# A third place for split weights, and what moves with it, in a two-block transformer kernel on one core

## The chip, the cores and the metric

The kernel runs on one core of one Trainium2 chip. The metric is the device time of one execution in microseconds (us). One execution takes about 2.1 ms. TensorE (PE) multiplies, VectorE (DVE) and ScalarE (ACT) work elementwise, GpSimd (POOL) does little here, SyncE (SP) does nothing but wait and issue transfers. The five run from their own instruction lists, in order, and meet at semaphores.

## The reference, cut to what matters

Float32 in and out, 256 tokens of 2048 channels. The first block is a mixer, a cross attention and a mixture of 16 experts. The second block has two layers, and most of the change lies in them:

```python
for l in range(2):
    mod = silu(c) @ w_ada[l] + b_ada[l]            # 2048 x 6144: a product with one row
    shift, scale, gate = split(mod, 3)
    h = rmsnorm(x, norm_g[l]) * (1 + scale) + shift
    z = h @ w_in[l]                                # 2048 x 6656: 13 pieces of 512
    o_fft  = fourier_mix(f_x, w_fft[l]) * silu(f_g)
    o_na   = neighbourhood_attention(na_q, na_k, na_v, bias[l]) * silu(na_g)
    o_ret  = retention(rotary(r_q), rotary(r_k), r_v) * silu(r_g)
    o_cv   = conv31_layernorm_silu(cv_a, cv_b) @ w_pw[l] * silu(cv_g)
    x = x + gate * (concat(o_fft, o_na, o_ret, o_cv) @ w_out[l])

def rotary(t):                                     # t1, t2: the halves of a head of 64
    return concat(t1 * cos - t2 * sin, t1 * sin + t2 * cos)
```

## The kernel before, in words

**Blocks of weights.** Every large product runs over blocks of 128 x 2048 float32 (1 MB). SP loads a block into one of four raw places (`raw`, rooms 0 to 3, line 471). ACT writes its high half as float16 (line 644), DVE the low half (line 1292, which also gives the raw place back, `raw_taken`), and PE multiplies x-high by w-high, x-low by w-high and x-high by w-low: 48 matmuls for a block (line 2241). The halves have two places (`SPL = 2`, `w_hi`, `w_lo`), so ACT may start on block m only when PE is done with block m - 2 (`block_done`).

**The order of the stream.** `STREAM` lists the phases: `w_in` (40 blocks), `w_out`, `wk`, `wq`, `wv`, `wo` (16 each), `moe` (192 blocks, in rings of their own and up to eight raw places), then for each of the two layers `z` (52 blocks, 4 for each of the 13 pieces in `Z_ORDER`) and `mix` (16). `raw_rooms` (line 125) gives each block the raw place that was used longest ago. Two small weight matrices of a layer sit in the same stream and hold a raw place unsplit until PE has used them: `w_fft` after block 43 of `z`, used at block 45 (`fft_map`, lines 2805 to 2818), and `conv_w_pw` after block 48 (`small`, line 2839).

**The modulation units.** The product with `w_ada` is done on DVE: 12 units of 16 steps, each step 128 x 1024 float32 (0.5 MB), loaded by SP into one of two staging buffers (line 476, `load_ada`, which waits until the step two before is used) and added with one instruction of DVE (line 1263). `ada_plan` (line 144) says after which block a step comes. In `z` the steps of the first unit come after blocks 2 to 13 and those of the second unit after the blocks up to 29. DVE does a step right behind its split of that block, inside `split` (line 1285). SP's list is fixed too: load of block m, then the steps that belong to block m - 2 (`load_due(2)`, line 482), then, after block 43, `w_fft`.

**What else DVE and PE do within `z`.** DVE applies 120 taps of the convolution (`TAPS_AT`, line 2008), the attention's maxima, the rotary of q and k (`rotary`, line 2038, blocks 28, 30, 32, 34), weights of the retention, `conv_centre` at 41, `conv_squares` at 42, `na_gate` and `fft_weights` (lines 2076, 2101, 2102) at 43, `conv_norm` and `mixed_lo` (lines 2068 to 2071 and 2124) at 44. PE does `rotate(j)` (line 2740: a float32 product with a 128 x 128 permutation, into bank 2 of `GB`), scores, transposes and small products between the blocks; at 45, ahead of the block, it does `ret_square_sum` (line 2773) and `fft_map`.

**Start of the experts.** PE gathers the sorted rows in 16 products, DVE copies the low part of each (line 1867), ACT the high part (line 976), and the first expert's product takes them one by one.

Of the kernel before, what the change touches and what calls it, by code (L numbers as in the profile page):

```python
# [14 lines left out]
P = 128  # L15
T = 256
# [8 lines left out]
SPL = 2  # L25
# [24 lines left out]
Z_UNITS = (7, 8, 10, 11)  # L50
# [4 lines left out]
TAPS_AT = {**{m: 4 for m in range(11, 20)}, 20: 6, 21: 3, 22: 5, 23: 6, 24: 3, 25: 5, 26: 6, 27: 3, 28: 3, 29: 6, 30: 2,  # L55
           31: 6, 32: 2, 33: 6, 34: 3, 35: 4, 36: 4, 37: 4, 38: 7}
# [5 lines left out]
def constants():  # L62
# [13 lines left out]
    out["rope_cos"], out["rope_sin"] = np.cos(rope), np.sin(rope)  # L76
    rot = np.zeros((P, P))
    for m in range(P):
        if m % DH < half:
            rot[m + half, m] = -1.0  # L80
        else:
            rot[m - half, m] = 1.0
    out["rot"] = rot
# [41 lines left out]
def raw_rooms():  # L125

    (first, _, n), total = places()["moe"], sum(n for _, n, _ in STREAM)
    rooms, uses, last = [], [0] * ROOMS, [-1] * ROOMS
    for b in range(total):
        j = b - first  # L130
        open_ = list(range(RAW))
        if 0 <= j < n:
            open_ += [4] * (j >= 6) + [5] * (7 <= j < 126) + [6] * (j >= 7) + [7] * (13 <= j < 150)
        r = min(open_, key=lambda r: last[r])
        uses[r], last[r] = uses[r] + 1, b
        rooms.append((r, uses[r]))
    return rooms
# [6 lines left out]
def ada_plan():  # L144
# [21 lines left out]
    fast("z0")  # L166
    for m in [2, 2, 3, 4, 4, 5, 6, 6, 7, 8, 8, 9, 9, 10, 10, 11]:
        put("mix0", m)
    fast("z1")
# [27 lines left out]
def build(nc, A, table, const_at, columns, router, out):  # L197
    ctx = ExitStack()
    with ctx:
# [21 lines left out]
        w_hi = sb("w_hi", [P, SPL, BLK], F16)  # L221
        w_lo = sb("w_lo", [P, SPL, BLK], F16)
# [30 lines left out]
        hid_at = [H[:, k * 1024:(k + 1) * 1024] for k in range(4)] + [Zf[:, c * T:c * T + 1024] for c in (28, 48)] + [Yf[:, k * 1024:(k + 1) * 1024] for k in range(2)]  # L253
        raw_at = [raw[:, r, :] for r in range(RAW)] + [w3, Yf[:, 0:BLK], Yf[:, BLK:2 * BLK], Zf[:, 40 * T:48 * T]]
# [32 lines left out]
        RO = Y[:, 5:7, :]  # L287
        f_parts = w2[:, 0:1024].rearrange("p (a k g n) -> p a k g n", a=TT, k=2, g=4)
        f_last = w2[:, 1024:1032].rearrange("p (a g) -> p a g", a=TT)
# [8 lines left out]
        LO_AT = {"ga": 0, "weight": KC, "t": KC + 1, "y": KC + 1 + 4 * TILES}  # L298
# [61 lines left out]
        def ada_sums(u):  # L360
            if u in Z_UNITS:
                return Zf[:, (4 * (u in (8, 11))) * T:(4 * (u in (8, 11)) + 4) * T]
# [13 lines left out]
        def ada_bank(u):  # L376
            return MB[:, 0, 0:8] if u in (8, 11) else GB[:, 2, 0:8]
# [42 lines left out]
        def done(eng, ph, j, i=0):  # L420

            s = where(ph, j)[1]
            eng.wait_ge(block_done[s % SPL], s // SPL + 1 + 2 * i)
# [31 lines left out]
        def _(sp):  # L455
# [5 lines left out]
            def load(ph, j, src):  # L461
                r, n = rooms[where(ph, j)[0]]
                if n > 1:
                    sp.wait_ge(raw_taken[r], n - 1)
                elif r == 4:
# [12 lines left out]
            ADA_ROOM = {"w_out": ("hgrn_y", 2), "z0": ("norm_ms", 4), "mix0": ("small_mm", 2), "z1": ("norm_ms", 5)}  # L478

            due = []  # L480

            def load_due(depth):

                while len(due) > depth:
# [3 lines left out]
                    for step in steps:  # L488
                        load_ada(step)
# [66 lines left out]
        def _(gp):  # L556
# [64 lines left out]
        def _(act):  # L621
            def split_half(ph, j, half):
# [7 lines left out]
                act.activation(w_hi[:, s % SPL, cut], raw_at[r][:, cut], ACT.Copy, scale=W_SCALE).then_inc(hi_done, 1)  # L630

            def split(ph, j, i=0):
# [3 lines left out]
                if ph == "moe":  # L636
                    act.wait_ge(block_done[s % SPL], s // SPL - 1)
# [3 lines left out]
                else:  # L641
                    act.wait_ge(block_done[s % SPL], s // SPL + 2 * i)
                    w = w_hi[:, s % SPL, :]
# [369 lines left out]
            for n in range(MOE_STEPS):  # L1013
                f, last = n // 8, n % 8 == 7
                for part in range(2):
# [19 lines left out]
                    if n == 2 and part == 1:  # L1035
# [205 lines left out]
        def _(dve):  # L1241
# [23 lines left out]
            def ada_add(u):  # L1265
                dve.wait_ge(ada_mm, u + 1)
                mod = MOD[:, u // 6, u % 6 * 8:u % 6 * 8 + 8]
                if u % 6 < 4:
# [5 lines left out]
                    ("z0", 20): 7, ("z0", 33): 8, ("mix0", 14): 9, ("z1", 20): 10, ("z1", 33): 11}  # L1274

            def split_half(ph, j, half):
# [4 lines left out]
                ins = dve.scalar_tensor_tensor(w_lo[:, s % SPL, cut], raw_at[rooms[b][0]][:, cut], W_SCALE, w_hi[:, s % SPL, cut], ALU.mult, ALU.subtract)  # L1281
# [3 lines left out]
            def split(ph, j, i=0):  # L1285
                b, s = where(ph, j)
                dve.wait_ge(hi_done, s + 1 + 4 * i + (s > at["z1"][1]))
                hi, lo = w_hi[:, s % SPL, :], w_lo[:, s % SPL, :]
# [576 lines left out]
            def gather_lo(c):  # L1865
                dve.wait_ge(S("moe_mm"), MM_AT["ga"] + c + 1)
                dve.tensor_copy(xs_lo[:, c, :], gather_bank(c, 1)).then_inc(S("moe_lo"), 1)  # L1867
# [32 lines left out]
            for n in range(MOE_STEPS):  # L1900
                f, last = n // 8, n % 8 == 7
                for part in range(2):
# [23 lines left out]
                    if part == 1:  # L1926
                        if n == 0:
                            groups_left()
                        if n == 2:
# [3 lines left out]
                        if n in (3, 4):  # L1933
                            place_rows(n - 3)
# [41 lines left out]
            for l in range(LAYERS):  # L1976
# [244 lines left out]
        def _(pe):  # L2221
            def product(ph, j, b, k0, start, stop, groups=None, x=(xh, xl), rows=False, between=None):

                s = at[ph][1] + j
                hi = w_hi[:, s % SPL, :].rearrange("p (c n) -> p c n", c=8)
                lo = w_lo[:, s % SPL, :].rearrange("p (c n) -> p c n", c=8)
# [767 lines left out]
```

## Time and profile before

| what | us |
|---|---|
| median of 3 runs | 2095.44 |
| lowest and highest run | 2094.69, 2101.43 |
| the profiled execution: its own time | 2093.71 |
| its span, first to last instruction | 2091.7 |
| PE busy | 2041.4 |
| DVE busy | 1752.3 |
| ACT busy | 1194.1 |

The span is 2.0 us shorter than the profiled execution's own time, and that is 1.7 us under the median. The stages in the trace: `w_in` 17 to 266 us, `w_out` to `wo` until 725, experts 725 to 1233, `z` of the first layer 1247 to 1573, its `mix` to 1660, `z` of the second layer 1667 to 1994, its `mix` to 2078. Busy times are unions; the idle time of an engine stands with what ended it, as the trace infers it from the semaphores.

### The profile page before, as it was taken

The numbers are of one execution on the slowest core, as the hardware profiler recorded it, in microseconds if no ns is written. First come the engines' busy times: TensorE is split into PE (matmuls) and PEld (weight loads), VectorE is DVE, ScalarE is ACT, GpSimd is POOL, SyncE is SP. The second block draws the span as 40 slices with busy tenths as digits, with TensorE's granted clock in tenths as the row PEclk, the third lists the DMA queues.
The fourth block names the chain that finished last, engine by engine and source line by source line (L and its number), as shares of the span: only waits on it lengthen the run. The fifth ranks groups of instructions, "written<-read, shape, count | busy, mean of one in ns | idle before, by whom it ended". The sixth has DMA issues, their size and how long they took to land.

```text
span 2091.7 us, 42599 instructions
## 1 busy us (share of the span) xinstructions
PE 2041.4 (98%) x18993; PEld 1641.1 (78%) x18993; DVE 1752.3 (84%) x1670; ACT 1194.1 (57%) x1071; POOL 41.3 (2%) x40
## 2 busy tenths in 40 slices
PE   8999999999999989999999999999999899999998
PEld 7889888888889946555556568888888788888887
DVE  7875787988888799999999999999668779996555
ACT  5554644444445478877877864456554444565543
POOL 0002300000000000000000000000000000000000
PEclk9999999999999999999999999999999999999999
DMA  8854487789888878999999987874458778744452
GB/s 303 317 202 162 163 314 271 280 307 326 319 326 298 309 280 355 420 420 420 420 420 416 408 318 293 294 256 164 143 184 310 281 286 304 250 162 159 181 202 101
DMA packets 95717, 593.23 MB, mean 284 GB/s; under 512 B 10664, under 2 KB 10824, under 8 KB 36784
## 3 DMA queue, kind: packets, MB, share of 16 engines
q1 hardware_dynamic: 94912, 583.73, 74.4%
q0 software_dynamic: 624, 6.80, 0.8%
q8 instruction: 149, 2.44, 0.5%
q14 instruction: 32, 0.26, 0.0%
HBM read 588.39 MB, written 2.10 MB: 282 GB/s over the span
## 4 chain that ended last, share of the span: by engine, by line
PE 68%; DVE 16%; DMA 10%; ACT 3%; issue 3%; DVEq 0%; SPq 0%; POOL 0%; ACTq 0%; POOLq 0%
PE GB L2241 52%; DVE w_lo L1292 6%; PE GB L2670 4%; DVE W L1292 3%; PE MB L2670 3%; DMA raw<-w_up 3%; DMA W<-w_ada 2%; ACT w_hi L644 2%; DMA Z<-w_ada 2%; DMA raw<-w_down 2%; DVE W L1263 1%; DVE Z L1263 1%; DMA raw<-w_gate 1%; PE MB L2839 1%; PE MB L2441 1%
## 5 line engine op out<-in xcount | busy, mean ns | idle before, releaser
L644 ACT ACTIVATE w_hi<-raw 128x2048 f16<-128x2048 f32 x308 | 588.1, 1910 | 705.5 <-PE GB L2241 680.9
L1292 DVE SCALAR_TENSOR_TENSOR w_lo<-raw,w_hi 128x2048 f16<-128x2048 f32 x308 | 706.0, 2294 | 244.9 <-ACT w_hi L644 244.2
L2241 PE MATMUL GB<-H,w_hi 128*128 128x256 f16 x4352 | 718.9, 273 | 18.3 <-DVE w_lo L1292 11.6
L2241 PE MATMUL GB<-H,w_lo 128*128 128x256 f16 x2176 | 593.8, 273 | 0.0
L2241 PEld LDWEIGHTS GB<-H,w_hi 128*128 128x128 f16 x4352 | 421.6, 98 | 85.0 <-DVE w_lo L1292 16.6
L2241 PEld LDWEIGHTS GB<-H,w_lo 128*128 128x128 f16 x2176 | 213.2, 98 | 24.9
L2241 PE MATMUL GB<-w_hi,H 128*128 128x256 f16 x1280 | 210.7, 273 | 0.0
L1263 DVE SCALAR_TENSOR_TENSOR W<-W,SM 128x1024 f32<-128x1024 f32 x120 | 153.8, 1282 | 31.8 <-DMA W<-w_ada 28.5
L2241 PE MATMUL GB<-w_lo,H 128*128 128x256 f16 x640 | 174.4, 273 | 0.0
L2241 PE MATMUL GB<-Z,w_hi 128*128 128x256 f16 x1024 | 170.0, 274 | 2.9 <-DVE w_lo L1292 2.9
L2241 PE MATMUL GB<-W,w_hi 128*128 128x256 f16 x1024 | 168.0, 273 | 2.7 <-DVE w_lo L1292 2.7
L2241 PE MATMUL GB<-Z,w_lo 128*128 128x256 f16 x512 | 140.4, 274 | 0.0
L2241 PE MATMUL GB<-W,w_lo 128*128 128x256 f16 x512 | 139.6, 273 | 0.0
L2241 PEld LDWEIGHTS GB<-w_hi,H 128*128 128x128 f16 x1280 | 124.7, 98 | 16.1 <-issue 1.3
L1292 DVE SCALAR_TENSOR_TENSOR W<-raw,W 128x2048 f16<-128x2048 f32 x54 | 123.2, 2286 | 2.3 <-ACT W L644 2.2
L644 ACT ACTIVATE W<-raw 128x2048 f16<-128x2048 f32 x54 | 103.0, 1911 | 20.9 <-DMA raw<-w_down 6.1
L2241 PEld LDWEIGHTS GB<-Z,w_hi 128*128 128x128 f16 x1024 | 100.4, 98 | 16.0 <-DVE w_lo L1292 3.8
L2241 PEld LDWEIGHTS GB<-W,w_hi 128*128 128x128 f16 x1024 | 99.9, 98 | 14.9 <-DVE w_lo L1292 3.3
L2008 DVE SCALAR_TENSOR_TENSOR Y<-Y,PC 128x256 f32<-128x256 f32 x240 | 99.6, 479 | 0.0
L2670 PE MATMUL GB<-W,Z 128*64 (+1 forms) x864 | 86.7, 353 | 4.4 <-DVE Z L1867 4.3
L2670 PE MATMUL MB<-W,Z 128*64 (+1 forms) x864 | 86.0, 353 | 1.3 <-DVE W L1292 1.2
L1263 DVE SCALAR_TENSOR_TENSOR Z<-Z,SM 128x1024 f32<-128x1024 f32 x60 | 76.8, 1281 | 10.7 <-DMA Z<-w_ada 9.9
(489 smaller groups left out, 2789.9 us busy)
## 6 DMA issues: line engine op xcount, KB each, us to landing
raw<-w_in SPq DMA_DIRECT2D x144, 1024.0 KB, 5.2
W<-w_ada SPq DMA_DIRECT2D x128, 512.0 KB, 5.6
raw<-w_out SPq DMA_DIRECT2D x48, 1024.0 KB, 5.1
raw<-w_down SPq DMA_DIRECT2D x41, 1024.0 KB, 10.6
raw<-w_gate SPq DMA_DIRECT2D x34, 1024.0 KB, 11.0
raw<-w_up SPq DMA_DIRECT2D x32, 1024.0 KB, 12.8
Z<-w_ada SPq DMA_DIRECT2D x64, 512.0 KB, 5.9
raw<-xattn_wk SPq DMA_DIRECT2D x16, 1024.0 KB, 5.1
```

The costliest lines, as they stand in the source:

```text
L644: act.activation(w, raw_at[r], ACT.Copy, scale=W_SCALE).then_inc(hi_done, 1)
L1263: dve.scalar_tensor_tensor(sums, w, SM[:, 24 + k:25 + k], sums, ALU.mult, ALU.add).then_inc(ada_used[n % 2], 1)
L1292: dve.scalar_tensor_tensor(lo, raw_at[r], W_SCALE, hi, ALU.mult, ALU.subtract).then_inc(raw_taken[r], 1)
L2008: dve.scalar_tensor_tensor(ca[:, c, :], CU[:, c, k // 4:k // 4 + T], col("conv_w_2", l * TAPS * 4 + k), ca[:, c, :], ALU.mult, ALU.add).th ...
L2241: last = pe.matmul(o, a, m, start=first, stop=end and w_part is lo, skip_group_check=True)
L2441: ins = pe.matmul(MB[:, h % 2, a * T:a * T + T], x_q[q][:, 4 * h + c, a * P:a * P + P], x_k[k][:, 4 * h + c, :], start=a == 0 and c == 0 a ...
L2670: ins = pe.matmul(o_bank(j, k)[r:r + SLOT], x[:, c0 + c, at_:at_ + SLOT], v, start=kh == 0 and c == 0 and part == 0, stop=kh == 7 and c == ...
L2839: ins = pe.matmul(banks[:, n // 2, n % 2 * T:n % 2 * T + T], w[:, k, n * P:n * P + P], x[:, k, :], start=n % 2 == 0 and k == 0, stop=k == ...
```

## The change

1. `SPL = 3`: the halves get a third place. It is cut out of raw place 3, so outside the experts the blocks of the stream use raw places 0 to 2 only; within the experts place 3 opens at the fifth block. ACT may now start on block m when PE is done with block m - 3.
2. The steps of each `z`'s second modulation unit move from blocks 14 to 29 to blocks 35 to 46; those of the first unit are spread up to block 16. The products that finish the units move to blocks 19 and 50. Staging and sums of the second unit get other buffers (`w2`, `w3`), and the spectrum's parts move from `w2` to `w1`.
3. The taps are dealt out again over blocks 11 to 37 (120 as before).
4. The rotary partner is moved by POOL: four transfers of 32 partitions x 512 float32 for each of the four pairs of pieces, in place of `rotate`. The sign goes into the table of sines. DVE's three instructions stay, the first reads SBUF in place of PSUM.
5. At the start of the experts ACT copies the low part of the odd gathers, DVE only of the even ones; `groups_left`, `best_two` and `place_rows` come a step or two later.

```diff
-SPL = 2
+SPL = 3
-Z_UNITS = (7, 8, 10, 11)
+Z_UNITS = (7, 10)
-TAPS_AT = {**{m: 4 for m in range(11, 20)}, 20: 6, 21: 3, 22: 5, 23: 6, 24: 3, 25: 5, 26: 6, 27: 3, 28: 3, 29: 6, 30: 2,
-           31: 6, 32: 2, 33: 6, 34: 3, 35: 4, 36: 4, 37: 4, 38: 7}
+TAPS_AT = {11: 5, 12: 4, 13: 6, 14: 4, 15: 6, 16: 4, 17: 6, 18: 6, 19: 6, 20: 6, 21: 6, 22: 2, 23: 6, 24: 6, 25: 2, 26: 6, 27: 6, 28: 2, 29: 4, 30: 6, 32: 6, 33: 2, 34: 6, 35: 2, 36: 3, 37: 2}
...
-        open_ = list(range(RAW))
+        open_ = list(range(RAW - 1))
         if 0 <= j < n:
-            open_ += [4] * (j >= 6) + [5] * (7 <= j < 126) + [6] * (j >= 7) + [7] * (13 <= j < 150)
+            open_ += [3] * (j >= 4) + [4] * (j >= 6) + [5] * (7 <= j < 126) + [6] * (j >= 7) + [7] * (13 <= j < 150)
...
-    def fast(ph):
-        for m in [2 + 2 * k // 3 for k in range(13)] + list(range(11, 30)):
+    def halves(ph):
+        for m in [2, 2, 3, 4, 4, 5, 6, 6, 7, 8, 8, 9, 10, 12, 14, 16]:
+            put(ph, m)
+        for m in [35, 36, 37, 37, 38, 39, 39, 40, 41, 41, 42, 42, 43, 44, 45, 46]:
             put(ph, m)
...
+        third = raw[:, RAW - 1, :].bitcast(F16)
+        hi_of = [w_hi[:, 0, :], w_hi[:, 1, :], third[:, 0:BLK]]
+        lo_of = [w_lo[:, 0, :], w_lo[:, 1, :], third[:, BLK:2 * BLK]]
...
+                for j in range(4):
+                    for u in range(j % 2 + 1):
+                        gp.wait_ge(bank_free[u], uses[f"z{l}"][u] + 6 + j // 2)
+                    if j == 0:
+                        gp.wait_ge(S("tap"), 4 * TAPS * l + 4)
+                    if j == 3:
+                        gp.wait_ge(S("rotated"), 4 * l + 1)
+                    if l or j:
+                        gp.wait_ge(S("rot"), 64 * (4 * l + j))
+                    for d in range(0, P, DH // 2):
+                        s = d ^ DH // 2
+                        gp.dma_start(RO[j % 3][d:d + DH // 2], Z[s:s + DH // 2, 24 + 2 * j:26 + 2 * j, :]).then_inc(S("rot"), 16)
...
             def gather_hi(c):
                 act.wait_ge(S("moe_mm"), MM_AT["ga"] + c + 1)
+                if c % 2:
+                    act.activation(xs_lo[:, c, :], gather_bank(c, 1), ACT.Copy)
                 act.activation(xs_hi[:, c, :], gather_bank(c, 0), ACT.Copy).then_inc(S("moe_hi"), 1)
...
                 def rotary(j):
                     x = Z[:, 24 + 2 * j:26 + 2 * j, :]
-                    dve.wait_ge(S("rot"), 4 * l + j + 1)
-                    link(dve.tensor_tensor(RO, GB[:, 2, :].rearrange("p (c t) -> p c t", t=T), sin, ALU.mult))
+                    dve.wait_ge(S("rot"), 64 * (4 * l + j + 1))
+                    ro = RO[j % 3]
+                    link(dve.tensor_tensor(ro, ro, sin, ALU.mult))
                     link(dve.tensor_tensor(x, x, cos, ALU.mult))
-                    dve.tensor_tensor(x, x, RO, ALU.add).then_inc(S("rotated"), 1)
+                    dve.tensor_tensor(x, x, ro, ALU.add).then_inc(S("rotated"), 1)
...
-                def rotate(j):
-                    evicted(pe, l, 5 + j // 2)
-                    if j == 0:
-                        pe.wait_ge(ada_mod, 8 + 3 * l)
-                    else:
-                        pe.wait_ge(S("rotated"), 4 * l + j)
-                    pe.matmul(GB[:, 2, :], const("rot"), Z[:, 24 + 2 * j:26 + 2 * j, :].rearrange("p c t -> p (c t)"), start=True, stop=True).then_inc(S("rot"), 1)
-
...
-                    if m == 17:
+                    if m == 19:
                         ada_columns(7 + 3 * l)
-                    if m == 32:
-                        pe.wait_ge(S("na_max"), 8 * l + 8)
+                    if m == 50:
+                        pe.wait_ge(S("fft_act"), 7 * l + 7)
                         ada_columns(8 + 3 * l)
-                    for j in nth(m, 27, 2):
-                        rotate(j)
```

## Rows read from the trace of the kernel before

**Rows 1.** The page: busy time of each engine, share of the span, instructions.

```profile
PE 2041.4 (98%) x18993; PEld 1641.1 (78%) x18993; DVE 1752.3 (84%) x1670; ACT 1194.1 (57%) x1071; POOL 41.3 (2%) x40
```

**Rows 2.** Waits of PE, whole span: who waited for whom, total, times, longest.

```profile
PE GB L2241 <- DVE w_lo L1292: 17.3, 20, 2.1
PE GB L2670 <- DVE Z L1867: 5.2, 5, 1.6
```

**Rows 3.** The same view, 0 to 50 us.

```profile
PE GB L2241 <- DVE w_lo L1292: 2.8, 3, 1.9
```

**Rows 4.** The same view, 265 to 280 us.

```profile
PE GB L2241 <- DVE w_lo L1292: 2.1, 1, 2.1
```

**Rows 5.** Chain that ended last, around blocks 43 to 46: start, us, what.

```profile
1510.17 0.43 PE GB L2829 x2
1510.60 10.48 PE GB L2241 x96
1521.08 1.72 PE MB L2773 x4
...
1528.17 0.66 PE GB L2818 x4
1528.83 0.14 issue
1528.96 10.64 PE GB L2241 x96
```

**Rows 6.** SP's list in order of time, at the end of `fft_map`.

```profile
1528.84 0.80 SPq L471 DMA_DIRECT2D raw<-w_in  x2
```

**Rows 7.** ACT in order of time, within block 41.

```profile
1491.74 0.43 ACT L1140 ACTIVATE NS<-GB 128x256 f32<-128x256 f32 x1
1496.14 1.91 ACT L644 ACTIVATE w_hi<-raw 128x2048 f16<-128x2048 f32 x1 [3.97 <-PE GB L2241]
```

**Rows 8.** DVE in order of time, blocks 42 to 45.

```profile
1500.30 0.68 DVE L1995 TENSOR_TENSOR Z<-Y 128x512 f32<-128x512 f32 x1
1501.02 0.42 DVE L1996 TENSOR_TENSOR Z<-Z 128x256 f32<-128x256 f32 x1
1503.33 2.29 DVE L1292 SCALAR_TENSOR_TENSOR w_lo<-raw,w_hi 128x2048 f16<-128x2048 f32 x1 [1.89 <-ACT w_hi L644]
1505.54 0.42 DVE L2059 COPY Z<-GB 128x256 f32<-128x256 f32 x1
...
1508.26 1.23 DVE L2102 TENSOR_TENSOR raw<-raw 128x1024 f32<-128x1024 f32 x1
...
1514.42 1.75 DVE L2068 RECIPROCAL NS<-NS 128x256 f32<-128x256 f32 x1
...
1519.89 2.28 DVE L1292 SCALAR_TENSOR_TENSOR w_lo<-raw,w_hi 128x2048 f16<-128x2048 f32 x1
```

**Rows 9.** Line 476, 352 to 381 us, `w_ada` loads close behind a block's.

```profile
DMA to landing us min/median/max: 3.5/5.7/6.5
```

**Rows 10.** Line 476 again, 1262 to 1325 us.

```profile
DMA to landing us min/median/max: 3.5/5.2/7.8
```

**Rows 11.** Line 1263: engine, count, duration min/median/max in ns.

```profile
L1263 DVE SCALAR_TENSOR_TENSOR Z<-Z,SM x60: 1275/1280/1286, 1263.9 to 1835.7; 128x1024 f32<-128x1024 f32 x60
```

**Rows 12.** Stretches: length, busy of PE, PEld, DVE, ACT, POOL, clock, DMA.

```profile
36.24:38.18 1.94, 0.01 (x1) 0.01 (x1) 1.94 (x2) 1.93 (x3) 0.00 (x0) 1.00 1.01 416
38.62:42.03 3.41, 3.41 (x18) 2.35 (x16) 3.29 (x3) 0.82 (x3) 0.00 (x0) 0.50 0.99 393
270.91:272.96 2.05, 0.00 (x1) 0.00 (x0) 2.05 (x2) 2.02 (x3) 0.00 (x0) 1.00 0.00 0
274.14:277.54 3.40, 3.40 (x18) 2.44 (x17) 3.40 (x3) 0.92 (x1) 0.61 (x1) 0.50 0.84 341
```

**Rows 13.** Chain that ended last, 1402 to 1412 us: one rotation.

```profile
1402.54 0.86 PE GB L2740 x2
```

**Rows 14.** Line 1867: the copies of the gathered low parts.

```profile
L1867 DVE CAST Z<-MB x16: 616/618/625, 735.8 to 789.9; 128x448 f16<-128x448 f32 x16
```

**Rows 15.** Stretches: blocks 22 to 34, 35 to 45 of `z`, and two in the experts.

```profile
1368.00:1456.00 88.00, 87.43 (x770) 72.47 (x767) 86.93 (x127) 53.36 (x87) 0.00 (x0) 1.00 0.58 200
1456.00:1529.00 73.00, 72.85 (x620) 61.04 (x618) 52.22 (x55) 44.69 (x46) 0.00 (x0) 1.00 0.37 127
...
930.00:1230.00 300.00, 291.71 (x2960) 166.59 (x2958) 285.64 (x155) 241.06 (x159) 0.00 (x0) 1.00 1.01 414
```

**Rows 16.** POOL's small transfers (line 564): issue in ns, then landing.

```profile
L564 POOL DMA_DIRECT2D LG<-ret_logit_fwd x1: 555/555/555, 10.6 to 10.6; - x1
...
DMA to landing us min/median/max: 7.0/7.2/7.4
```

**Rows 17.** DVE in order of time: the last rotation's first instruction.

```profile
1446.79 0.68 DVE L2041 TENSOR_TENSOR Y<-GB,CT 128x512 f32<-128x512 f32 x1
```

More of the change, by code:

```diff
@@ L75, in constants @@
     rope = (t.astype(np.float32)[None, :] * inv[p % half][:, None]).astype(np.float32)
[L76 to L80, printed above, removed]
-        else:
-            rot[m - half, m] = 1.0
-    out["rot"] = rot
+    out["rope_cos"], out["rope_sin"] = np.cos(rope), np.sin(rope) * np.where(p % DH < half, -1.0, 1.0)[:, None]
     d = t[None, :] - t[:, None]
@@ L165, in ada_plan @@
         put("wo", m)
-    fast("z0")
+    halves("z0")
     for m in [2, 2, 3, 4, 4, 5, 6, 6, 7, 8, 8, 9, 9, 10, 10, 11]:
         put("mix0", m)
-    fast("z1")
+    halves("z1")
     assert count[0] == 12 * ADA_STEPS
@@ L220, in build @@
         raw = sb("raw", [P, RAW, BLK])
-        w_hi = sb("w_hi", [P, SPL, BLK], F16)
-        w_lo = sb("w_lo", [P, SPL, BLK], F16)
+        w_hi = sb("w_hi", [P, 2, BLK], F16)
+        w_lo = sb("w_lo", [P, 2, BLK], F16)
         XT = sb("XT", [P, KC, T])
@@ L286, in build @@
         ca, csq, cs = Y[:, 12:16, :], Y[:, 8:12, :], Z[:, 12:14, :]
-        RO = Y[:, 5:7, :]
-        f_parts = w2[:, 0:1024].rearrange("p (a k g n) -> p a k g n", a=TT, k=2, g=4)
-        f_last = w2[:, 1024:1032].rearrange("p (a g) -> p a g", a=TT)
+        RO = [Y[:, 5 + 2 * k:7 + 2 * k, :] for k in range(3)]
+        f_parts = w1[:, 0:1024].rearrange("p (a k g n) -> p a k g n", a=TT, k=2, g=4)
+        f_last = w1[:, 1024:1032].rearrange("p (a g) -> p a g", a=TT)
         f_cos, f_nyq, f_sin = Zf[:, 0:2 * MIRROR], Zf[0:4, 2 * MIRROR:3 * MIRROR], Zf[:, 2 * T:2 * T + 2 * MIRROR]
@@ L376, in ada_bank @@
         def ada_bank(u):
-            return MB[:, 0, 0:8] if u in (8, 11) else GB[:, 2, 0:8]
+            return MB[:, 0, 0:8] if u in Z_UNITS else GB[:, 2, 0:8]
         def na_p(h):
@@ L464, in load @@
                     sp.wait_ge(raw_taken[r], n - 1)
+                elif r == RAW - 1:
+                    done(sp, "wo", 13)
                 elif r == 4:
@@ L488, in load_due @@
                     for step in steps:
+                        if step in LATE_ROOM:
+                            sp.wait_ge(S("na_o"), LATE_ROOM[step])
                         load_ada(step)
@@ L629, in split_half @@
                 cut = slice(half * BLK // 2, half * BLK // 2 + BLK // 2)
-                act.activation(w_hi[:, s % SPL, cut], raw_at[r][:, cut], ACT.Copy, scale=W_SCALE).then_inc(hi_done, 1)
+                act.activation(hi_of[slot(s)][:, cut], raw_at[r][:, cut], ACT.Copy, scale=W_SCALE).then_inc(hi_done, 1)
             def split(ph, j, i=0):
@@ L636, in split @@
                 if ph == "moe":
-                    act.wait_ge(block_done[s % SPL], s // SPL - 1)
+                    act.wait_ge(block_done[(s - 4) % SPL], (s - 4) // SPL + 1)
                     if j < 2:
@@ L641, in split @@
                 else:
-                    act.wait_ge(block_done[s % SPL], s // SPL + 2 * i)
-                    w = w_hi[:, s % SPL, :]
+                    act.wait_ge(block_done[s % SPL], s // SPL)
+                    if (ph, j) == ("z0", 0):
+                        given_up(act, RAW - 1)
+                    w = hi_of[slot(s)]
                 act.activation(w, raw_at[r], ACT.Copy, scale=W_SCALE).then_inc(hi_done, 1)
@@ L1034, in _ @@
                             turned_hi(n // 16 - 1, k)
-                    if n == 2 and part == 1:
+                    if n == 3 and part == 1:
                         act.wait_ge(S("r_exp_in"), 1)
@@ L1926, in _ @@
                     if part == 1:
-                        if n == 0:
+                        if n == 2:
                             groups_left()
-                        if n == 2:
+                        if n == 3:
                             best_two()
@@ L1932, in _ @@
                             combine()
[L1933 to L1934 removed]
+                        if n in (4, 6):
+                            place_rows(n // 2 - 2)
                     if n == 6 and part == 1:
```

35 lines of the change are left out of this document (19 added, 16 removed).

## The prediction, made before the changed kernel ran

> **What bounds the kernel now.** I read the engines' shares first: PE is busy for 98% of the span, and its clock is at full speed in all but a few stretches [rows 1]. So a microsecond taken off PE's own list is a microsecond of the time, and a microsecond by which something keeps PE waiting is one too. Next the waits of PE: the largest entry is its wait for the low halves that DVE makes, 17.3 us in 20 waits, and after it 5.2 us for DVE's copies of gathered rows [rows 2]. Then the chain that ended last, in `z`: PE runs blocks of 48 matmuls in 5.24 us with small products between them, and nothing else is on it [rows 5]. DVE has 98% of blocks 22 to 34 filled, but only 72% of blocks 35 to 45 [rows 15]. Last I followed SP's list against the raw places, for the change takes one of four away.
>
> **Part 1, the rotations leave PE.** Each takes 0.86 us of PE's chain [rows 13], eight of them: 6.9 us off. DVE keeps its three instructions. The partner now comes by POOL's queue: four issues of 0.56 us and a landing of at most 7.4 us, so some 9.6 us a round by the nearest rows [rows 16]. Four rounds are 38 us. ACT gives the first piece away at about 1386 and the fourth at about 1418; the last round lands about 1428 and DVE wants it at 1446.8 [rows 17], or a block (5 us) earlier if it runs ahead. Cover: 13 us. Price taken: nothing.
>
> **Part 2, the third place of halves.** With two places a split may be late by 0.9 us at most: block 5.24, less 1.91 for the high half, 2.29 for the low half and the hand-overs [rows 5, 7, 8]. With three it may be late by 6.2 us. The 17.3 us of waits hold two that have other causes: 2.8 us at the start, where the norm feeds the blocks [rows 3], and 2.1 us at 271, where ACT stands behind a gate's result [rows 4]. That leaves 12.4 us. After each of the 16 waits PE takes a little to refill, so I take 14 us off. The bounds: 6, if DVE's lateness behind `w_ada` data comes back in part, and 17.
>
> **Part 3, the experts' start.** DVE loses eight copies of 0.62 us [rows 14] and PE its 5.2 us of waits for them at most [rows 2]. Most of the experts' stage runs at 414 GB/s with the transfers at their limit [rows 15], so an early start only counts as far as the transfers start early too. I take 3 us off, between 0 and 5.2.
>
> **Part 4, the moved unit.** Sixteen steps of 1.28 us [rows 11] leave the stretch in which DVE is 98% full for one with 21 us free in 73 [rows 15]; 20.5 us more there is less what the taps took with them (12 taps fewer). As work it fits. As an order of waits it does not, and this is where I put the time. Follow the raw places. With three, each block's load waits for the split of the block three ahead of it in the stream, and `w_fft` counts as a block that is given back only when `fft_map` ends. So block 46 follows `w_fft`. SP's list has the steps of block 44 behind the load of block 46, those of 43 behind 45, those of 42 behind 44. And since `w_fft` lies between, loads 44 and 45 wait for the splits of blocks 42 and 43, the very ones behind which DVE waits for the steps' data. Before, no step came after block 29, so nothing hung on this; in before's trace it is the load of block 47 that goes out as `fft_map` ends, at 1528.84 [rows 5, 6].
>
> *Block 44.* In before's times: ACT is free at 1492.2 [rows 7]; 1.9 for the high half, 2.3 for the low, so block 42 is split at 1496.4. Load 44 goes, the two steps' loads follow 0.4 us behind, and land 5.7 us later [rows 9]: 1502.5. Two steps: 1505.1. The squares' sums, 1.1: 1506.2. Split 43: 1508.5. Again 6.1 us and one step: 1515.9. Then the copy, gate and `w_fft` sums, in before 1505.5 to 1509.5, 4.0 us: 1519.9. Split 44: 1522.2 [rows 8, 11]. PE wants block 44 at 1515.9 [rows 5]. PE waits 6.3 us. Bounds 1.9 (landings of 3.5 us [rows 9]) and 8.
>
> *Block 45.* `fft_map` ends, load 46 goes out, and 0.4 us behind it the step of block 44. It lands at 6.1 us, the step ends at 7.4; only then may DVE do the norm of the convolution and the low part behind it, in before 1514.4 to 1519.9, 5.5 us, and then split 45, 2.3 [rows 8, 9, 11]. PE, which in before goes straight on at 1528.96 [rows 5], waits 15.0 us. Queued behind that step on DVE are all these; on SP, behind the blocked load 46, are loads 47, 48 and `conv_w_pw`; by my walk they come in time. Bounds 12.8 and 17.1, by landings of 3.5 and 7.8 us [rows 10]. Both waits come in both layers: 2 x 21.3 = 42.6 us on.
>
> *The clock.* After PE had stood still for 1.94 and for 2.05 us its granted clock fell from 1.00 to 0.50 (2.4 to 1.2 GHz) for 3.41 and 3.40 us [rows 12], which costs half of that, 1.7 us. Four long waits: 6.8 us on; bounds 3.4 and 13.6.
>
> **The sum** against the profiled execution: 2093.7 - 6.9 - 14 - 3 + 42.6 + 6.8 = 2119.2, rounded to 2119 (the median of the runs shown is 1.7 above that execution, which is within the rounding of the terms). The low ends together: 2093.7 - 6.9 - 17 - 5.2 + 29.4 + 3.4 = 2097. The high ends: 2093.7 - 6.9 - 6 + 0 + 50.2 + 13.6 = 2145.
>
> **Rivals.** *A, the room does not bind.* The loads of blocks 44 to 46 and the steps behind them come in time, because the given-back places run ahead of what I walk through. For it: PE in before had no wait at all in blocks 35 to 46 [rows 15], and the third place lets splits run a block early. Against it: no early split helps a load that waits for `fft_map`. Then only the gains stand: 2093.7 - 23.9 = 2070. It decides where the two waits of a layer fall below 12 us together: from there the gains win. *B, POOL's transfers are late.* DVE is busy for 86.9 of 88 us there [rows 15], and if that holds up POOL's transfers, a round takes longer than by the rows of the kernel's start. It binds from about 15 us a round; at 19 us the last lands 16 us too late, in both layers: 2119 + 32 = 2151. The Trainium skill has the mechanism (SBUF — State Buffer, section "SBUF: two separate sides"): it says that GpSimd cannot write the descriptors of its own transfers while certain VectorE instructions hold the port pair that they share. No run here shows it for the rotary. *C, the third place gives nothing*, because DVE's lateness comes from the `w_ada` data itself, two staging buffers deep, and three raw places let SP issue those a block later: 2119 + 14 = 2133. *D, the change doesn't act as described*, for instance the halves' third place is never free in time, with nothing lost: 2095.
>
> **Chances.** Forecast (both waits in both layers, gains as taken) 0.66; A 0.12; B 0.05; C 0.13; D 0.04. C lies within the forecast's bounds, so does most of what could shift a term. I leave A and B out: the range is 2097 to 2141. A measurement of this kernel can tell about 0.3%, 6 us, from no change. Faster by more than that: A, 0.12. Within it: D and the low corner of the forecast, 0.07. Slower: 0.81.
>
> **What would show it.** In the changed profile: no line 2740, and 0.86 us less at four places of each `z`; PE's waits for the low halves in `w_in` to `wo` and in `mix` near nothing; in each `z` a wait of PE of some 6 us ahead of block 44 and some 15 us ahead of block 45, ended by DVE's split, with DVE waiting ahead of line 1263's instruction for a `w_ada` transfer issued just after `fft_map`; the granted clock at 0.50 behind each. If PE is without a wait there, the walk along the raw places is wrong and the time is near 2070. If DVE waits ahead of the rotation's first instruction, it is B.

## The result, and the profile after

The changed kernel took 2198.0 us (median of four runs, 2196.0 to 2203.8) against 2095.1 us: a ratio of 1.049, 95% interval 1.046 to 1.052. The direction and the place of the long waits were as forecast; the size was four times as large, +103 us where +24 had been forecast, and far outside the range of 2097 to 2141 us.

The profiled execution took 2203.8 us, 110 more than the one of before. The page, part 1 (busy time of each engine, its share of the span, instructions), beside [rows 1]:

```profile
PE 2061.3 (94%) x18977; PEld 1645.2 (75%) x18977; DVE 1751.7 (80%) x1662; ACT 1196.0 (54%) x1079; POOL 58.1 (3%) x72
```

PE lost its share of the span, DVE did the same work as before (1752 us). PE was busy 20 us longer with 16 instructions fewer, at a mean granted clock of 0.976 where it had been 0.994. The other 90 of the 110 us are idle time of PE: it waited. Whom PE waited for (total, times, longest), beside [rows 2]:

```profile
PE GB L2266 <- DVE w_lo L1315: 72.5, 41, 15.0
PE GB L2266 <- DVE raw L1315: 31.7, 16, 15.1
```

Both lines are the same split on DVE; the third place of halves lies in `raw`, hence the second name. Together 104 us, where 17.3 had been. What did the splits wait for? The same view of DVE, first for after, then for before:

```profile
DVE W L1286 <- DMA W<-w_ada: 198.9, 82, 21.6
DVE Z L1286 <- DMA Z<-w_ada: 33.2, 20, 3.7
```

```profile
DVE W L1263 <- DMA W<-w_ada: 28.5, 33, 1.8
DVE Z L1263 <- DMA Z<-w_ada: 9.9, 9, 2.7
```

In these lines DVE stood still for `w_ada` data for 232 us where it had been 38. The question is where this reached PE. The table takes the stretches between the ends of blocks' last matmuls in the two profiled executions, in us (the first column up to block 39 of `w_in`, the experts up to their last block):

```
                   w_in  w_out..wo  experts  z:0-20   21-35   36-42   43-45   46-51   mix
before  layer 0   265.7      459.3    508.3   131.8    96.0    49.1    24.2    38.7   87.4
after   layer 0   272.4      479.7    510.6   141.3    91.4    49.1    56.1    39.1   94.5
before  layer 1                               125.0    96.2    49.1    24.2    39.2   83.8
after   layer 1                               133.3    91.4    49.1    57.1    39.1   83.8
```

Blocks 43 to 45 lost 31.9 and 32.9 us: that is the place of the forecast. But `w_in` to `wo` lost 27 us (1.2 of them before the first block's end, with no step near), blocks 0 to 20 of `z` lost 9.5 and 8.3, and `mix` of layer 0 lost 7.1: 52 us in stages from which the forecast took its gain. The last `mix` has no step of `w_ada`, and it is the same to 0.1 us. Only blocks 21 to 35 gained, 4.6 and 4.8 us. Blocks 36 to 42 have eleven steps since the change and lost nothing: with the small products between them PE takes 7.0 us for a block there (49.1 for seven), not 5.24.

**Blocks 43 to 45** look as the walk along the raw places said. DVE in order of time (start, us, line, operation; in brackets the idle time before it and who ended it):

```profile
1541.04 2.69 DVE L1286 SCALAR_TENSOR_TENSOR W<-W,SM 128x1024 f32<-128x1024 f32 x2 [6.30 <-DMA W<-w_ada]
...
1544.71 2.28 DVE L1315 SCALAR_TENSOR_TENSOR w_lo<-raw,w_hi 128x2048 f16<-128x2048 f32 x1
1554.73 1.28 DVE L1286 SCALAR_TENSOR_TENSOR W<-W,SM 128x1024 f32<-128x1024 f32 x1 [7.74 <-DMA W<-w_ada]
...
1559.80 2.28 DVE L1315 SCALAR_TENSOR_TENSOR w_lo<-raw,w_hi 128x2048 f16<-128x2048 f32 x1
1583.67 1.28 DVE L1286 SCALAR_TENSOR_TENSOR W<-W,SM 128x1024 f32<-128x1024 f32 x1 [21.59 <-DMA W<-w_ada]
1584.88 1.74 DVE L2093 RECIPROCAL NS<-NS 128x256 f32<-128x256 f32 x1
...
1590.35 2.28 DVE L1315 SCALAR_TENSOR_TENSOR raw<-raw 128x2048 f16<-128x2048 f32 x1
```

These are the splits of blocks 43, 44 and 45, each with a late step ahead of it. The third step's data were sent for just after `fft_map` had ended. SP's list in order of time:

```profile
1547.02 0.33 SPq L475 DMA_DIRECT2D raw<-w_in  x1
1547.39 0.43 SPq L480 DMA_DIRECT2D W<-w_ada  x1
1577.60 0.33 SPq L475 DMA_DIRECT2D raw<-w_in  x1
1577.98 0.43 SPq L480 DMA_DIRECT2D W<-w_ada  x1
```

PE's longest waits in these stretches (layer 0, then layer 1):

```profile
PE GB L2266 <- DVE raw L1315: 15.1, 1, 15.1
PE GB L2266 <- DVE w_lo L1315: 11.2, 2, 9.7
```

```profile
PE GB L2266 <- DVE w_lo L1315: 21.4, 2, 15.0
PE GB L2846 <- DVE Z L2020: 3.6, 1, 3.6
```

**Everywhere else** the same thing happens in small. `w_out`, DVE:

```profile
296.03 2.28 DVE L1315 SCALAR_TENSOR_TENSOR w_lo<-raw,w_hi 128x2048 f16<-128x2048 f32 x1
298.51 2.69 DVE L1286 SCALAR_TENSOR_TENSOR W<-W,SM 128x1024 f32<-128x1024 f32 x2 [0.20 <-DMA W<-w_ada]
301.11 2.28 DVE L1315 SCALAR_TENSOR_TENSOR raw<-raw 128x2048 f16<-128x2048 f32 x1
306.38 1.28 DVE L1286 SCALAR_TENSOR_TENSOR W<-W,SM 128x1024 f32<-128x1024 f32 x1 [2.98 <-DMA W<-w_ada]
...
308.18 2.28 DVE L1315 SCALAR_TENSOR_TENSOR w_lo<-raw,w_hi 128x2048 f16<-128x2048 f32 x1
```

and SP:

```profile
298.34 0.33 SPq L475 DMA_DIRECT2D raw<-w_out  x1
299.82 0.33 SPq L480 DMA_DIRECT2D W<-w_ada  x1
303.42 0.33 SPq L475 DMA_DIRECT2D raw<-w_out  x1
```

Read it as a ring. The split of block 4 ends at 298.31 and gives its raw place back. At 298.34 the load of block 7, three ahead, goes out. Behind it stands the step of block 5; its transfer is issued at 299.82, when a staging buffer comes free too, and DVE starts on the data at 306.38. The step is done at 307.7, and the split of block 6 ends at 310.46. That is two blocks in 12.15 us, where PE needs 10.48 for two. The stretch (length, busy of PE, PEld, DVE, ACT, POOL, clock, DMA share, GB/s):

```profile
298.31:310.46 12.15, 10.65 (x96) 9.31 (x96) 8.86 (x7) 3.42 (x3) 0.00 (x0) 1.00 0.78 278
```

PE stood still for 1.5 of the 12.15 us and DVE for 3.3, so no engine was the bound: the ring itself was. In before, with four places, the same ring goes from a split to the third one after it and has three blocks' time, 15.7 us.

### The profile page after: what moved, and what is told of

It reads as the page before. It is cut to its first block, busy times and chain, and to the rows that moved or that the text cites. A ratio compares the mean times of both kernels' runs of the same rounds, so it can differ in the third digit from the quotient of the medians.

```text
span 2202.0 us, 42604 instructions
## 1 busy us (share of the span) xinstructions
PE 2061.3 (94%) x18977; PEld 1645.2 (75%) x18977; DVE 1751.7 (80%) x1662; ACT 1196.0 (54%) x1079; POOL 58.1 (3%) x72
## 4 chain that ended last, share of the span: by engine, by line
PE 27%; DVE 27%; DMA 26%; issue 16%; ACT 4%; SPq 1%; POOLq 0%; POOL 0%; DVEq 0%; ACTq 0%
PE GB L2266 16%; DMA W<-w_ada 14%; DVE w_lo L1315 8%; DVE W L1286 4%; DMA Z<-w_ada 4%; PE GB L2695 3%; PE MB L2695 3%; DVE W L1315 3%; DMA raw<-w_up 3%; DVE raw L1315 3%; DMA raw<-w_down 2%; ACT w_hi L665 2%; DMA raw<-w_gate 1%; DVE Z L1286 1%; DVE Y L2032 1%
## 5 line engine op out<-in xcount | busy, mean ns | idle before, releaser
L1315 DVE SCALAR_TENSOR_TENSOR w_lo<-raw,w_hi 128x2048 f16<-128x2048 f32 x223 | 511.1, 2295 | 80.8 <-ACT w_hi L665 79.9
L665 ACT ACTIVATE w_hi<-raw 128x2048 f16<-128x2048 f32 x223 | 425.0, 1906 | 209.9 <-PE GB L2266 97.6
L2266 PE MATMUL GB<-H,w_hi 128*128 128x256 f16 x2880 | 482.5, 275 | 51.0 <-DVE w_lo L1315 48.9
L2266 PE MATMUL GB<-H,w_lo 128*128 128x256 f16 x1440 | 395.4, 275 | 0.0
L2266 PEld LDWEIGHTS GB<-H,w_hi 128*128 128x128 f16 x2880 | 280.1, 99 | 98.5 <-DVE w_lo L1315 55.8
L2266 PE MATMUL GB<-H,raw 128*128 128x256 f16 x2208 | 257.1, 277 | 30.2 <-DVE raw L1315 26.8
L2266 PEld LDWEIGHTS GB<-H,raw 128*128 128x128 f16 x2208 | 217.3, 100 | 67.6 <-DVE raw L1315 31.0
L1315 DVE SCALAR_TENSOR_TENSOR raw<-raw 128x2048 f16<-128x2048 f32 x85 | 195.3, 2298 | 22.9 <-ACT raw L665 22.6
L665 ACT ACTIVATE raw<-raw 128x2048 f16<-128x2048 f32 x85 | 161.9, 1905 | 94.0 <-PE GB L2266 46.5
L2266 PEld LDWEIGHTS GB<-H,w_lo 128*128 128x128 f16 x1440 | 142.0, 99 | 17.4
```

The costliest lines, as they stand in the source:

```text
L665: act.activation(w, raw_at[r], ACT.Copy, scale=W_SCALE).then_inc(hi_done, 1)
L1315: dve.scalar_tensor_tensor(lo, raw_at[r], W_SCALE, hi, ALU.mult, ALU.subtract).then_inc(raw_taken[r], 1)
L2266: last = pe.matmul(o, a, m, start=first, stop=end and w_part is lo, skip_group_check=True)
```

## The experiments

Theory L ("the list"), formed after the result: what costs is how many blocks lie between the split that lets a load go and the split that waits for the `w_ada` data behind that load in SP's list. The change made them two instead of three. Ratios below are against the kernel before on the same chip, with their 95% interval.

**Three raw places alone.** `open_ = list(range(RAW - 1))` and `[3] * (j >= 4)` for the experts, the rest as before.

> The kernel before with three raw places outside the experts in place of four, and nothing else: two places of halves, its own plan of w_ada steps, its product for the rotary. Theory L (the list): a load waits for the low half of the block three back instead of four back, and the w_ada loads of the block two back stand behind it in SP's list, so they go out a block later; DVE, which wants them in order, waits for data, and its next low half is late. L expects DVE's waits for w_ada to grow from 41 us to over 150 us, PE's waits for low halves to grow from 17 us to some 60 us, and a time of 2140 to 2160 us. Rival H (the third place of halves or DVE's own work is what costs, not the raw place): the time stays within 6 us of the kernel before, 2095.

Measured: 2174.6 us, ratio 1.036 (1.033 to 1.040). A raw place alone costs more than L had said: PE's waits for low halves grew to 75 us, where L had said some 60. DVE's waits for `w_ada` data grew to 149 us, just under L's number. Rival H falls.

**Three raw places and three places of halves.** As above, with the changed kernel's `third`, `hi_of`, `lo_of` and `slot`.

> The kernel before with three raw places and three places of halves, nothing else of the change. L expects the third place of halves to give back some of what the raw place costs, since a late low half is covered by one block more of made halves: 2125 to 2145 us, clearly below the kernel with three raw places and two of halves, yet above the kernel before. The forecast's term (third place of halves gives 14 us off and the raw place costs nothing outside blocks 44 and 45) expects 2081 us. Rival H expects it no faster than the one with two places of halves.

Measured: 2167.6 us, ratio 1.034 (1.032 to 1.037), some 23 us above L's range. By the medians the third place of halves gave back 7 us, but the two intervals overlap, so a gain is not shown. The forecast's term (2081 us) is out. DVE waits for the steps' data no less than with two places of halves (149 us in these two lines, 144 there):

```profile
DVE W L1275 <- DMA W<-w_ada: 111.0, 68, 4.4
DVE Z L1275 <- DMA Z<-w_ada: 38.1, 31, 2.8
```

A likely reason, which no run tests by itself: a store of made halves covers a single late split, but where every pair of blocks takes longer than PE the store is soon empty.

**The order of SP's list, in the changed kernel.**

```diff
-                        load(ph, m, ...)
                         due.append((ph, plan.get(ph, {}).get(m, [])))
                         load_due(2)
+                        load(ph, m, ...)
```

> The changed kernel with one thing moved: SP issues the w_ada loads of the block two back ahead of a block's load instead of behind it, in every linear stage. L expects nearly all of the loss to go: the 27 us by the end of wo, the 65 us at blocks 44 and 45 of both layers and most of the 18 us in the first twenty blocks of z and in mix; 2080 to 2095 us, DVE's waits for w_ada under 60 us. A rival W (DVE's own work, or the two staging buffers of w_ada, hold the splits up) expects the waits to stay: 2170 us or more. A third, S (the loads of w_ada now hold up the loads of the blocks, since they wait for their staging buffers): 2110 to 2140 us.

Measured: 2095.3 us, ratio 1.000 (0.998 to 1.001). One line takes all of the 103 us away. The time lies 0.3 us above the range that L had named. PE's waits:

```profile
PE GB L2266 <- DVE w_lo L1315: 10.5, 7, 5.5
PE GB L2266 <- DVE raw L1315: 8.8, 4, 4.1
```

W falls (DVE's work and the two staging buffers are the same here), S too. L had DVE's waits for `w_ada` data wrong: it said under 60 us, and they are 93 us (81 in `W`, 11 in `Z`). PE's waits above show that most of them no longer reach it.

**The same only from block 42 of `z` on** (`late = ph in ("z0", "z1") and m >= 42`).

> The changed kernel with the same order of SP's list only from block 42 of each z on. L expects only the long waits ahead of blocks 44 and 45 to go, with the slow clock behind them: these two stretches were 64.8 us longer than in the kernel before, so 2133 us, and the rest of the loss, some 40 us, stays. If w_fft's place itself is what holds the stretch up (the load of block 46 after fft_map), the waits move to blocks 46 and 47 and the time is 2150 to 2175 us.

Measured: 2146.2 us, ratio 1.025 (1.021 to 1.028): 52 us off instead of 65. Blocks 43 to 45 are at 24.2 us again in both layers, as in before, so the waits there did hang on the list. The time lies between L's 2133 us and the 2150 of the other expectation, for both were at work. But blocks 46 to 51 took 47.2 and 45.0 us, against 38.7 and 39.2. That is the remark on `w_fft`'s place: PE now waited 5.6 and 4.1 us for block 46, whose load still goes out when `fft_map` ends. The kernel with three raw places alone, which has no step near, shows it too (44.9 and 45.0).

**The list changed by one number, with all four raw places.** The kernel before with `load_due(3)` for `load_due(2)`.

> The kernel before, all four raw places and two places of halves, with one number changed: SP issues the w_ada loads of a block behind the load of the block three further on, not two. Nothing is taken away, no work is added. L says that the raw place as such is not what matters, only how many blocks lie between the split that lets a load go and the split that waits for the w_ada data behind it: with four places and a distance of three these are two blocks, as with three places and a distance of two. L expects nearly the loss that the kernel with three places showed outside fft_map, some 65 us: 2150 to 2170 us. If a raw place less costs by the weights' own lateness (loads of blocks landing late), this kernel stays within 10 us of 2095.

Measured: 2164.8 us, ratio 1.031 (1.028 to 1.034), within what L said. Nothing was taken away and no work added; two blocks of distance do it. `w_out` to `wo` took 488.1 us (489.8 with three raw places alone, 459.3 before), blocks 46 to 51 of the first `z` 38.7 (44.9): the loss along the list is there, that at `w_fft`'s place is not. PE's and DVE's waits:

```profile
PE GB L2241 <- DVE w_lo L1292: 69.1, 62, 3.0
```

```profile
DVE W L1263 <- DMA W<-w_ada: 107.8, 69, 3.1
DVE Z L1263 <- DMA Z<-w_ada: 41.5, 31, 3.2
```

**Control: the new order in the kernel before.**

> The kernel before with only the order of SP's list changed, as a control: four raw places, two of halves. With four raw places each w_ada load already has three blocks of time; L expects 2090 to 2096 us, less only where DVE waited for w_ada data (41 us in all, most of them not on the path). If the new order is a gain by itself, whatever the places, it should show here as 2085 us or less, and then it is no proof for L.

Measured: 2096.0 us, ratio 1.000 (0.998 to 1.002), as L said. With four places the order is worth nothing that shows.

**Three raw places, three places of halves and the new order**, no other part.

> The kernel before with three raw places, three places of halves, and the w_ada loads ahead of the block's load in SP's list; no other part of the change. L expects the loss of the kernel with halves alone (72 us over the kernel before) to go in the stages with w_ada steps and the third place's gain to show there, some 12 us of PE's waits; what stays is the stretch after fft_map, which in the kernels with three raw places took about 6 us more per layer in blocks 46 to 51 with no w_ada step near, since the load of block 46 waits for w_fft's place. Together 2095 - 12 + 12 = 2095 us, 2088 to 2100. If the order were not the cause of the loss, 2150 us or more.

Measured: 2099.2 us, ratio 1.001 (1.000 to 1.002), within L's range and 68 us less than without the order. Against the control, `w_out` to `wo` are 2.5 us shorter and the first `mix` 3.2, while blocks 46 to 51 are 6.3 and 4.4 longer.

**The rotary by DMA alone**, on the kernel before.

> The kernel before with the rotary's partner moved by POOL's DMA in place of the product, and nothing else. The forecast's term: eight times 0.86 us, 6.9 us off, 2088 to 2089 us, if the transfers are hidden. The rival with POOL held up by DVE's instructions expects DVE to wait ahead of the rotation's first instruction and 2095 us or more.

Measured: 2096.6 us, ratio 1.001 (1.000 to 1.002): nothing, and neither expectation. The rival is out: DVE never sat idle ahead of the rotation's first instruction, in none of the eight rotations here and in none of the changed kernel's eight, and in the changed kernel the 32 transfers were issued in 0.50 us each and landed in 2.5 to 6.2 us. The products did leave PE. But blocks 21 to 35 took 95.3 and 95.5 us instead of 96.0 and 96.2, where four times 0.86 are 3.4. The stretch (length, busy of PE, PEld, DVE, ACT, POOL, clock, DMA share, GB/s):

```profile
1367.50:1462.70 95.20, 92.17 (x834) 78.15 (x831) 93.28 (x135) 58.24 (x88) 7.88 (x16) 1.00 0.62 215
```

DVE is busy for 93.3 of 95.2 us, PE for 92.2, and PE waited 2.1 us for a split at 1430. That DVE became the bound as soon as PE's list got shorter is argued from this row; the product put back, below, tests it.

**The gathers alone**, on the kernel before.

> The kernel before with every second low copy of the gathered rows on ACT and the router's work two steps later, and nothing else. The forecast's term was 3 us off, between 0 and 5.2: 2092 us. In the kernels run so far that had this part, the stretch from the end of wo to the last block of the experts was never shorter than before (508.2 to 510.6 us against 508.3). If what bounds that stretch is the transfers, an early start of PE gives nothing: 2095 us, within 0.2%.

Measured: 2092.7 us, ratio 0.998 (0.997 to 0.999), 3.8 us less by the medians and barely clear of nothing. The profiled execution does not say where: wo's end to the last experts' block is 508.6 us (508.3 before), and PE's waits for the low copies went from 5.2 us to one wait of 2.4, with one of 2.5 for a router step beside it. So the size agrees with the term, the place is not shown.

**`w_fft` one block later**, on the changed kernel with the new order: `FFT_AFTER, PW_AFTER = 44, 48`.

> The changed kernel with the w_ada loads ahead of the block's load, and w_fft's load one block later in the stream (behind block 44's, so that block 47's load and not block 46's takes its place when fft_map ends). In the kernel with the first of these alone, PE waited 5.5 and 4.1 us for block 46 and the stretch of blocks 46 to 51 took 7.4 and 6.3 us more than in the kernel before, partly at the slow clock. If w_fft's place is the cause, those 13.7 us go: 2082 us, 2078 to 2085. If the cause is DVE's list behind fft_map (the convolution's norm ahead of the split of block 46), they stay: 2094 to 2097 us.

Measured: 2083.6 us, ratio 0.995 (0.993 to 0.996). The waits for block 46 are gone; blocks 46 to 51 took 41.0 and 41.2 us. The rest over 38.7 and 39.2 is for the most part a wait for the next weight of the same kind:

```profile
PE MB L2856 <- DMA raw<-conv_w_pw: 3.6, 2, 1.9
```

**The rotary's product back**, in that kernel.

> The fastest kernel so far (the changed kernel with the w_ada loads ahead of the block's load and w_fft one block later, 2083.6 us) with the rotary's product back on PE in place of the DMA. The rotary by DMA on top of the kernel before gave nothing, and there PE waited 2.1 us for DVE within blocks 22 to 34. Theory R: the 0.86 us only count where DVE has room in these blocks, which the moved unit makes. R expects this kernel 6.9 us slower than the one it is made from: 2090 to 2091 us. If the product were hidden also here, 2083 to 2085 us.

Measured: 2090.8 us, ratio 0.997 (0.996 to 0.998), where R had said 2090 to 2091. That is 7.2 us more than with the DMA by the medians; the two kernels ran on different chips, and by the ratios it is 5 us with intervals that just overlap. The traces decide for R: blocks 21 to 35 took 94.8 us with the product and 91.4 without, 3.4 us in each layer. Here is the same stretch of the kernel with the DMA:

```profile
1365.20:1456.50 91.30, 91.30 (x818) 77.81 (x816) 80.92 (x118) 53.76 (x78) 7.88 (x16) 1.00 0.57 193
```

DVE is at 89% since the unit's sixteen steps left, and PE at 100%: here PE is the bound.

**The changed kernel without part 2**: four raw places, two of halves, old order.

> The changed kernel without its part 2: four raw places and two places of halves as in the kernel before; the moved unit, the rotary by DMA and the gathers in halves stay, and SP's order is the old one. L expects the whole loss to be tied to the raw place: no long wait ahead of blocks 44 and 45. By the walk along four places the step of block 45 now stands behind the load of block 47, which takes w_fft's place as fft_map ends, so DVE is 5 us late for block 46 in each layer. 2095 - 6.9 for the rotary + 2 x 5 and some slow clock: 2095 to 2105 us. If moving the unit is what costs, whatever the places, 2140 us or more.

Measured: 2099.2 us, ratio 1.001 (1.000 to 1.003), within L's range. So 99 of the 103 us were tied to part 2. PE's one long wait in the first layer's `z` stood ahead of block 46, 5.6 us at 1529.7 (4.2 in the second layer), and SP and DVE show the walk of the forecast one block further on:

```profile
1524.21 0.33 SPq L465 DMA_DIRECT2D raw<-w_in  x1
1524.58 0.43 SPq L470 DMA_DIRECT2D W<-w_ada  x1
```

```profile
1531.82 1.28 DVE L1274 SCALAR_TENSOR_TENSOR W<-W,SM 128x1024 f32<-128x1024 f32 x1 [13.08 <-DMA W<-w_ada]
1533.02 2.29 DVE L1303 SCALAR_TENSOR_TENSOR w_lo<-raw,w_hi 128x2048 f16<-128x2048 f32 x1
```

**The same with the new order.** What does the third place of halves give when nothing holds it back?

> The changed kernel without its part 2 (four raw places, two places of halves) and with the w_ada loads ahead of the block's load. Beside the fastest kernel so far (2083.6 us, three and three, the same order, w_fft one block later) it says what the third place of halves gives. With the old order it took 2099.2 us, with a wait of 5.6 and 4.2 us for block 46 in the two layers that this order should take away with its slow clock, some 13 us. If the third place gives most of the 14 us of the forecast, this kernel is near 2095; if it gives about the 6 us that the stages wk, wq and mix differ by, 2088 to 2091 us; if nothing, 2083 to 2086 us.

Measured: 2086.8 us, ratio 0.996 (0.995 to 0.998). So parts 1, 3 and 4 with the order give 8 us. The forecast's 14 us for the third place are out: that expectation was 2095 us for this kernel. The time lies between the other two, some 6 us and nothing. The kernel that differs by part 2 and the place of `w_fft` alone is the one of 2083.6 us. In both, block 47's load takes the place of `w_fft`, and blocks 46 to 51 are alike (41.0 and 41.0 us here). By the ratios it is 3 us faster, and the intervals overlap. A gain of the third place shows steadily in one stage only: the first `mix` took 84.2 to 84.7 us in the five kernels with three places of halves and the new order, and 87.4 to 89.3 in the six with four raw places and no loss along the list.

**`conv_w_pw` one block earlier** in the fastest kernel: `FFT_AFTER, PW_AFTER = 44, 47`.

> The fastest kernel so far with the load of conv_w_pw one block earlier in the stream as well, behind block 47's. In the fastest kernel PE waited 1.7 and 1.9 us for conv_w_pw, since its load waits for the split of the block three ahead. One block earlier it goes out a split earlier: the two waits go, 3.6 us off, 2080 us. If the loads of blocks 48 to 50 come later for it and PE waits for those, 2083 us or more.

Measured: 2079.8 us, ratio 0.993 (0.991 to 0.995), 15 us less than before and 118 less than the changed kernel: the fastest of all. In layer 1 0.5 us of the wait stayed and in layer 0 1.5 us, for which the trace names nobody; the 4 us that it lies below the kernel with only `w_fft` moved are not clear of the two intervals. Against the kernel without part 2 it is 7 us less, on the same chip. Not all of that is the third place, since `conv_w_pw` moved too (blocks 46 to 51 are 0.2 and 1.2 us shorter): 3 to 6 us are left for it, less than half of what the forecast gave. PE's waits for the low halves are 11.9 us here and were 15.8 in the other:

```profile
PE GB L2266 <- DVE w_lo L1315: 7.3, 8, 2.1
PE GB L2266 <- DVE raw L1315: 4.6, 3, 1.9
```

## Why the prediction was right and wrong

*Part 4 and the walk, right.* The wait ahead of block 45 was forecast as 15.0 us and was 15.1 and 15.0. Ahead of block 44, 6.3 had been forecast; PE lost 9.7 us there in layer 0 (with 2.0 more just before) and 6.3 in layer 1 (with 4.6 before, 3.6 of them for the convolution's sums, which stand behind the same late steps). The splits came into the stretch late already, which the walk in before's times had not. The slow clock behind the waits took another 12 us (64.8 us of longer stretches less 52.7 of waits), against 6.8 taken and 13.6 as bound. The granted clock agrees: it was at 0.50 in five stretches of the two layers, with 23.0 us of PE's work in them, and half of that is lost. Granted clock, stretch by stretch, at the second wait of layer 0:

```profile
1577.60:1580.50 2.90, 0.00 (x0) 0.00 (x0) 0.00 (x0) 0.00 (x0) 0.00 (x0) 1.00 0.65 186
1580.50:1597.50 17.00, 4.81 (x23) 3.47 (x24) 12.28 (x11) 10.78 (x8) 0.00 (x0) 0.50 0.59 231
1597.50:1600.50 3.00, 3.00 (x29) 2.64 (x28) 0.49 (x1) 0.00 (x0) 0.00 (x0) 0.99 1.02 426
```

After this wait it stayed at 0.50 for 4.8 us of work (4.9 to the end of the slow stretch), not 3.4. Together these stretches explain 65 of the 110 us; 49.4 had been forecast for them.

*Part 2, the step that failed.* The term "With three it may be late by 6.2 us", with 14 us off for it, counted only the halves' places, and took the raw place as free outside blocks 44 and 45. The walk along SP's list was made only where `w_fft` lies. Made in any stage with a step per block, it would have given, from rows of before: 0.4 to the issue, 5.7 the landing [rows 9], 1.3 the step [rows 11], 2.3 the split [rows 8], 0.7 for one small instruction between [rows 8], so 10.4 us for two blocks of 10.48. No slack is left where PE has nothing but blocks to do, and each second step in a block, each wait for a staging buffer and each landing of 6.5 us goes to PE. Where PE takes 7.0 us for a block, in blocks 36 to 42, the ring closes in time, and nothing was lost. Measured: 52 us lost in `w_in` to `wo`, `z` to block 20 and `mix`, in place of 12 to 14 gained. The forecast's own sign, waits for low halves near nothing in `w_in` to `wo`, failed: from 272 us to the end of `wo` they came to 21.6 us, more than the 17.3 of the whole span before. With the ring opened again by the order of the list, the third place gave 3 to 6 us. Rival C had the mechanism ("three raw places let SP issue those a block later") and priced it at a lost gain, 2133 us; it should have asked whether the ring still closes within PE's time. What came was C's mechanism at a much higher price, together with the forecast's own waits.

*Part 1.* The 6.9 us came out as 6.8 us in the traces in company of part 4 (7.2 by the medians, 5 by the ratios). Without it blocks 21 to 35 gained 1.4 us in both layers together and the time nothing. In the changed kernel both were there, and blocks 21 to 35 gained 4.6 and 4.8 us, 3.4 of them each by the rotary. The term was right because part 4 was there, and the forecast did not say so, though [rows 15] had DVE at 98%. POOL's transfers were hidden (rival B falls), and landed sooner than the rows of the start had said. The rule of the Trainium skill (SBUF — State Buffer, section "SBUF: two separate sides") is that GpSimd cannot write the descriptors of its transfers while VectorE runs an instruction in a two-port mode. The waits of these runs show no such hold-up; whether any instruction that DVE has in these blocks is of that kind is not shown.

*Part 3.* 3 us forecast; alone it measured 3.8. In the changed kernel the experts' stretch was 2.3 us longer. It was so with three raw places alone (510.7 against 508.3), but also in the control with four (511.3), so single profiles cannot say whether the place cost it.

*Rivals and range.* A (the room does not bind, 2070) and D fall. With the list in the new order, A's gains came only in part: 2095 with the order, 2080 with `w_fft` and `conv_w_pw` moved as well. The range's upper end, 2141, is not the 2145 that the sum of the high ends gives, and the forecast does not say why; [rows 1], cited for the clock at full speed, has no clock, which was 0.994 in the mean; 2198 lies above both. The upper sum left the third place a gain of 6 us at the least, where it needed a loss.

*What stays open.* Where the 3.8 us of the gathers lie, and how large the third place's gain is beyond the 3 to 5 us in the first `mix`. Single profiles differ by 1 to 3 us in `z` and the experts between kernels that are equal in those stages.

## What to carry to other kernels

Before a buffer is taken from a ring, walk once round the ring in the plainest stage: from the instruction that frees a place, through the in-order list behind the load that it lets go, to the instruction that waits for the last thing in that list. Divide by the blocks between; if that is near the bound engine's time per block, the buffer cannot go. A store further down the line did not make up for it here (2168 against 2175 us). Order the list by when things are wanted, not by what they belong to. And a saving on one engine counted here only as far as the next engine had room in that stretch: look for it there, not over the span.

## What the runs showed of the hardware

In the changed kernel the granted clock fell to 0.50 (1.2 GHz) in the midst of a 15.1 us wait, some 3 us after PE had stopped, and stayed so for 17.1 us, of which 4.9 were work; in the kernel before it had been 3.4 us after waits of 1.9 to 2.1 us [rows 12]. POOL's transfers of 32 rows within the on-chip memory landed in 1.8 to 5.6 us (median 3.0) in the kernel with the rotary alone, while DVE was busy for 98% of blocks 21 to 35; the small transfers at the kernel's start had taken 7.0 to 7.4 us [rows 16].
